# Gate projections cut into four parts over three attention passes, in place of two halves over two

## The chip, the cores and the metric

The kernel runs on one core of one Trainium2 chip. The metric is device microseconds (us), the median of three runs. TensorE is called PE below, VectorE DVE, ScalarE ACT, GpSimd POOL and SyncE SP.

## The reference, cut to what matters

Two transformer blocks in one launch: a first block with attention, a gated MLP mixer and a mixture of experts, and then a second block of two layers. The change stands in the token mixing of those two layers (`_token_mixing`, 256 tokens, width 1024):

```
proj = n @ w_in
nsa_q, nsa_kv, nsa_g, dil_qkv, fox_qkv, fox_f, merge_g = _split_cols(proj, IN_WIDTHS)
y_a = _nsa_attention(...)        # 4 heads: compressed, selected and windowed keys
y_b = _dilated_attention(...)    # 6 heads
y_c = _forgetting_attention(...) # 6 heads, scores plus a cumulated log gate
g_a, g_b, g_c = jnp.split(jax.nn.sigmoid(merge_g), 3, axis=-1)
merged = g_a * (y_a @ br_nsa) + g_b * (y_b @ br_dil) + g_c * (y_c @ br_fox)
return merged @ w_out
```

`merge_g` is 3 x 1024 columns of `n @ w_in`: the "gate units" below are the products that make it, 256 columns each, so 12 units in a layer. They need nothing of the attention, so they can stand between its steps.

## The kernel before

Every weight comes as a unit of 128 x 2048 float32 (1 MB) through a ring of three (`raw`, `whi`, `wlo`). SP loads a unit into `raw`; ACT rounds it (`conv_hi`, L278, `whi<-raw`); DVE subtracts to get the rest (`conv_lo`, L284, `wlo<-raw,whi`); PE then multiplies in three products, high by high, high by low and low by high (`mm3`, L357 to L359). A place of the ring can be converted anew once PE has used it (`unit_used`), and loaded anew once `conv_lo` has read it.

Each engine works through one list of instructions, written out by hand, in that order, and waits on semaphores. The part in question is the loop over 20 attention passes (one head each, both query tiles), with these steps for pass i:

- PE: scores of pass i into PSUM bank i % 2 (mask L2010, product L2016; the last six passes, those of the forgetting attention, have two more products, L2014), call it S(i); then three transposes of the exponentials of pass i-1 (L2025, T(i-1)), which wait for `exp2` of pass i-1; then the product with the values for pass i-2 (L2037, V(i-2)), which waits for `pt2_out`, ACT's copy of the transposed exponentials. Then the gate products of this pass, if any.
- DVE: the row maximum of pass i (L2423, R(i)); after it, in some passes, a `conv_lo`, or the closing arithmetic of a finished group of heads (`nsa_out` at 12, `dil_weights` at 15, `dil_out` at 18, `fox_out` at 19).
- ACT: the two exponentials of pass i (L2160, E(i)), which wait for R(i); in some passes the copy of a finished gate unit from bank 7 to its place (`gate_out`, L2102); the copy of the transposed pass i-1 (L2171); in some passes a `conv_hi`.

A gate unit is 48 products: two tiles of tokens, eight chunks of the depth, three products each. Six of the twelve units (numbers 5 to 10) stand in this loop and all use the one PSUM bank 7. A unit may start only when ACT has copied the unit before it out of the bank (`m_out`). The table of before and the waits around it:

```
ATT_GATES = {3 * (h // 2) + h % 2: (5 + h // 2, h % 2) for h in range(12)}
...
if tile == 0:
    pe.wait_ge(*(B["oc_out"].at(0, l) if f == 5 else B["m_out"].at(f - 1, l)))
gate_unit(f, 7, tile)
```

So three passes make a group: the first has 24 products of a unit, the second the other 24, the third none. ACT's `gate_out` and the conversion of the next unit (both engines) stand in the third pass of the group. After the loop come the last transposes of the outputs (`turn_two`, L1947), gate unit 11 in two halves, and the three branch products (units `BR0` to `BR0 + 2`).

Of the kernel before, what the change touches and what calls it, by code (L numbers as in the profile page):

```python
# [26 lines left out]
P = 128  # L27
# [3 lines left out]
DC = D // P  # L31
UNIT = 2048
RING = 3
# [93 lines left out]
def bass_network(nc, W, AD, x_in, ctx_in, s1_in, s2_in, k1_in, masks_in, gf_in, out):  # L127
    with ExitStack() as ctx:
# [17 lines left out]
        hhi = sb("hhi", [P, DC, S], F32R)  # L146
        hlo = sb("hlo", [P, DC, S], F32R)
# [23 lines left out]
        PS = ctx.enter_context(nc.psum_tensor("PS", [P, 8, 512], F32))  # L171
# [95 lines left out]
        def conv_hi(act, c, e=0):  # L267
            s = c % RING
            src = raw[:, s]
            if B1_UNITS <= c < LAYER0:  # L270
                m = c - B1_UNITS
                src = raw5[m % 5]
                act.wait_ge(landed5[m % 5], 16 * (m // 5 + 1))
            else:
                act.wait_ge(landed[s], e * 16 + 16 * ((c if c < LAYER0 else c - MOE_UNITS) // RING + 2))
            if not (isinstance(e, int) and c + 3 * e < RING):
                act.wait_ge(unit_used, e * 3 + (c - RING + 1))
            nc.scalar.activation(whi[:, s], src, ACT.Copy).then_inc(hi_ready, 1)  # L278

        def conv_lo(dve, c, e=0):  # L280
            s = c % RING
            dve.wait_ge(hi_ready, e * 3 + (c + 1))
            src = raw5[(c - B1_UNITS) % 5] if B1_UNITS <= c < LAYER0 else raw[:, s]
            nc.vector.tensor_tensor(wlo[:, s], src, whi[:, s].bitcast(F32), ALU.subtract).then_inc(lo_ready, 1)  # L284

        def unit(pe, c, e=0):
            pe.wait_ge(lo_ready, e * 3 + (c + 1))
            return whi[:, c % RING], wlo[:, c % RING]
# [66 lines left out]
        def mm3(out_, ah, al, bh, bl, start, stop, check=False):  # L355

            nc.tensor.matmul(out_, ah, bh, start=start, stop=False, skip_group_check=check)  # L357
            nc.tensor.matmul(out_, ah, bl, start=False, stop=False, skip_group_check=check)  # L358
            return nc.tensor.matmul(out_, al, bh, start=False, stop=stop, skip_group_check=check)  # L359
# [1508 lines left out]
        G = [qj[:, :, 256 * f:256 * f + 256] for f in range(5)] + [qj[:, :, C_FQ + 256 * f:C_FQ + 256 * f + 256] for f in range(3)]  # L1868
        G += [s1[:, 512 * f:512 * f + 512].rearrange("p (t n) -> p t n", t=2) for f in range(2)]
        G += [xn[:, :, 768:1024], oc_part.rearrange("p (t n) -> p t n", t=2)]  # L1870
        ATT_GATES = {3 * (h // 2) + h % 2: (5 + h // 2, h % 2) for h in range(12)}
        FF0, QK0 = LAYER0, LAYER0 + FFN_UNITS
        CM0 = QK0 + 15
        BR0 = QK0 + 26
# [1 line left out]
        CG = [QK0 + 12 + f + (2 if f >= 3 else 0) for f in range(12)]  # L1876
# [22 lines left out]
        def pe_layer(pe, l):  # L1899
# [35 lines left out]
            def gate_unit(f, bank, tile=None):  # L1935

                ins = project(unit(pe, CG[f], E0), hhi, hlo, bank, range(NT) if tile is None else (tile,))
                if tile != 0:
                    ins.then_inc(unit_used, 1)

            pe.wait_ge(*B["tb_act"].at(7, l))
# [63 lines left out]
            for i in range(PASSES2 + 2):  # L2005
                if i < PASSES2:
                    q, k, mk, _ = pass2(i)
                    if i >= 2:
                        pe.wait_ge(*B["exp2"].at(i - 2, l))
                    nc.tensor.matmul(PS[:, i % 2], idb[:, :], masks[:, mk], start=True, stop=False, skip_group_check=True)  # L2010
                    for t in range(NT):
                        o = PS[:, i % 2, 256 * t:256 * t + P * (t + 1)]
                        if i >= 14:
                            nc.tensor.matmul(o, fl[:, i - 14, t * P:(t + 1) * P], fr[:, 0:P * (t + 1)], start=False,  # L2014
                                             stop=False, skip_group_check=True)
                        ins = nc.tensor.matmul(o, q[:, t * P:(t + 1) * P], k[:, 0:P * (t + 1)], start=False, stop=t == 1,  # L2016
                                               skip_group_check=True)
                    ins.then_inc(*B["s2_mm"].up)
                if 1 <= i <= PASSES2:
                    p = i - 1  # L2020
                    pe.wait_ge(*B["exp2"].at(p, l))
                    if p >= 2:
                        pe.wait_ge(*B["pt2_out"].at(p - 2, l))
                    for n, c in enumerate((0, 256, 384)):
                        ins = nc.tensor.transpose(PS[:, 2 + p % 2, n * P:(n + 1) * P], pr2[:, p % 2, c:c + P], ident)  # L2025
                    ins.then_inc(*B["p2_turned"].up)
                if i >= 2:
                    p = i - 2
                    pe.wait_ge(*B["pt2_out"].at(p, l))
                    if p in (0, 4):  # L2030
                        pe.wait_ge(*B["m_out"].at(3 + p // 4, l))
                    if p == 12:
                        pe.wait_ge(*B["ya_done"].at(0, l))
                    bank, slot, v = FILL_BANK[p // 4], (p % 4) * 2, pass2(p)[3]
                    for t in range(NT):
                        for c in range(t + 1):
                            ins = nc.tensor.matmul(PS[:, bank, 64 * (slot + t):64 * (slot + t) + 64],  # L2037
                                                   pt2[:, p % 2, (t + c) * P:(t + c + 1) * P], qj[:, c, v:v + 64],
                                                   start=c == 0, stop=c == t)
                    ins.then_inc(*B["pv2"].up)  # L2040
                if i in ATT_GATES:
                    f, tile = ATT_GATES[i]
                    if tile == 0:
                        pe.wait_ge(*(B["oc_out"].at(0, l) if f == 5 else B["m_out"].at(f - 1, l)))
                    gate_unit(f, 7, tile)
                if i == PASSES2:
                    pe.wait_ge(*B["y2_made"].at(0, l))
                    turn_two(xn, 0, 6)
# [41 lines left out]
        def act_layer(act, l):  # L2090
# [8 lines left out]
            def gate_out(f, bank, conv=True):  # L2099

                act.wait_ge(unit_used, E0 * 3 + (CG[f] + 1))
                nc.scalar.activation(G[f], PS[:, bank].rearrange("p (t n) -> p t n", t=2), ACT.Copy).then_inc(*B["m_out"].up)  # L2102
                if conv:
                    conv_hi(act, CG[f] + RING, E0)
# [44 lines left out]
            for i in range(PASSES2 + 1):  # L2149
                if i < PASSES2:  # L2150
                    act.wait_ge(*B["negmax2"].at(i, l))
                    if i >= 2:
                        act.wait_ge(*B["p2_turned"].at(i - 2, l))
                    if i == 17:
                        act.wait_ge(*B["lse_sub"].at(0, l))
                        nc.scalar.activation(lw, lw, ACT.Exp).then_inc(*B["lse_exp"].up)
                    for t in range(NT):
                        n = 2 * i + t
                        o = slice(256 * t, 256 * t + P * (t + 1))
                        ins = nc.scalar.activation(pr2[:, i % 2, o], PS[:, i % 2, o], ACT.Exp, bias=nm2[:, n:n + 1],  # L2160
                                                   accum_out=den2[:, n:n + 1])
                    ins.then_inc(*B["exp2"].up)
                done = ATT_GATES.get(i - 1, (0, 0))
                if done[1]:
                    gate_out(done[0], 7, False)
                if i >= 1:
                    p = i - 1
                    act.wait_ge(*B["p2_turned"].at(p, l))
                    if p >= 2:
                        act.wait_ge(*B["pv2"].at(p - 2, l))  # L2170
                    nc.scalar.activation(pt2[:, p % 2, 0:384], PS[:, 2 + p % 2, 0:384], ACT.Copy).then_inc(*B["pt2_out"].up)  # L2171
                if done[1]:
                    conv_hi(act, CG[done[0]] + RING, E0)
            def split_hi(i, bank, dst):
                act.wait_ge(*B["y2_turned"].at(i, l))
                nc.scalar.activation(dst.rearrange("p c n -> p (c n)"), PS[:, bank], ACT.Copy).then_inc(*B["y2_hi"].up)
# [49 lines left out]
        def dve_layer(dve, l):  # L2226
# [194 lines left out]
            for i in range(PASSES2):  # L2421
                dve.wait_ge(*B["s2_mm"].at(i, l))
                nc.vector.tensor_reduce(nm2[:, 2 * i:2 * i + 2], PS[:, i % 2].rearrange("p (t n) -> p t n", t=2), AX.X, ALU.max,  # L2423
                                        negate=True).then_inc(*B["negmax2"].up)
                if i == 12:
                    nsa_out()
                done = ATT_GATES.get(i - 1, (0, 0))
                if done[1]:
                    conv_lo(dve, CG[done[0]] + RING, E0)
                if i == 15:  # L2430
                    dil_weights()
                if i == 18:
                    dil_out()
                if i == 19:
                    fox_out(14, 2, 4, 256)
# [306 lines left out]
```

## Time and profile before

| | |
|---|---|
| median of 3 runs | 2044.33 us (2043.84 to 2047.06) |
| the profiled execution, its own time | 2044.41 us |
| its span, first to last instruction | 2042.6 us |
| PE busy, of the span | 94% |
| DVE busy | 67% |
| ACT busy | 48% |
| mean granted PE clock | 0.975 |

PE is busy nearly all the time, so the total is PE's work and the few stretches in which it waits. In the rows further down a time is the start in us from the start of the span, and the number behind it is how long the merged piece lasted; the ends of matmuls are modelled and overlap the next start, so starts are what is compared. A square bracket gives the idle time of the engine ahead of the row and what ended it. "xN" is the count of merged instructions.

### The profile page before, as it was taken

How to read it: one execution, taken by the hardware profiler on the slowest of the kernel's cores; microseconds unless marked ns; L12 is line 12 of the kernel's file. 1: busy time of each engine (PE TensorE's matmuls, PEld its weight loads, DVE VectorE, ACT ScalarE, POOL GpSimd, SP SyncE). 2: the span in 40 equal slices, each digit the busy share in tenths (PEclk: the TensorE clock that was granted, in tenths of full speed). 3: DMA queues.
4: the chain of work that ended last, by engine and by line, in shares of the span. 5: the costliest groups of instructions: out<-in, count | busy, mean ns of one | idle time of the engine just before them, and what ended most of it. 6: DMA issues, size and time to landing. Idle time of an engine off the chain costs nothing.

```text
span 2042.6 us, 29838 instructions
## 1 busy us (share of the span) xinstructions
PE 1926.8 (94%) x12628; PEld 1717.0 (84%) x12656; DVE 1375.3 (67%) x1459; ACT 988.4 (48%) x1146; POOL 84.9 (4%) x107
## 2 busy tenths in 40 slices
PE   7999889999997999999998999999999999989998
PEld 3977678888886899899877899989998997779997
DVE  4889468898896777756336677678766462475444
ACT  3355457777775333454445533353335444444332
POOL 1330100000001000000000000000001000000000
PEclk9989989999998999999998999999999999899999
DMA  8556349999894687554321587748773542134554
GB/s 361 212 222 227 125 157 351 348 375 349 345 376 193 258 302 273 220 205 167 123 83 65 209 341 275 264 181 337 291 284 133 197 167 82 62 124 165 186 186 155
DMA packets 63878, 458.42 MB, mean 224 GB/s; under 512 B 7041, under 2 KB 7297, under 8 KB 8833
## 3 DMA queue, kind: packets, MB, share of 16 engines
q1 hardware_dynamic: 63744, 456.51, 59.1%
q8 instruction: 100, 1.64, 0.3%
q14 instruction: 34, 0.27, 0.0%
HBM read 455.43 MB, written 1.05 MB: 223 GB/s over the span
## 4 chain that ended last, share of the span: by engine, by line
issue 57%; PE 28%; DVE 9%; ACT 2%; DMA 1%; POOL 1%; DVEq 1%; POOLq 0%; ACTq 0%; SPq 0%
PE PS L357 8%; PE PS L359 7%; PE PS L358 7%; DVE acc L330 3%; DVE wlo L284 2%; PE PS L1253 1%; ACT whi L278 1%; PE PS L963 1%; DMA raw<-in_stream 1%; DMA ada<-in_ada 1%; POOL Z L489 1%; DVE hlo L466 0%; PE PS L935 0%; PE PS L1317 0%; DVE sm L1782 0%
## 5 line engine op out<-in xcount | busy, mean ns | idle before, releaser
L284 DVE TENSOR_TENSOR wlo<-raw,whi 128x2048 fp32r<-128x2048 f32 x282 | 646.8, 2296 | 349.2 <-ACT whi L278 344.0
L278 ACT ACTIVATE whi<-raw 128x2048 fp32r<-128x2048 f32 x282 | 538.5, 1912 | 359.1 <-PE PS L359 315.0
L357 PE MATMUL PS<-whi,hhi 128*128 128x256 f32 (+1 forms) x1568 | 504.8, 322 | 28.1 <-DVE wlo L284 13.3
L358 PE MATMUL PS<-wlo,hhi 128*128 128x256 f32 (+1 forms) x1568 | 493.1, 314 | 0.0
L359 PE MATMUL PS<-whi,hlo 128*128 128x256 f32 (+1 forms) x1568 | 492.9, 314 | 0.0
L357 PEld LDWEIGHTS PS<-whi,hhi 128*128 128x128 f32 x1568 | 304.8, 194 | 51.5 <-DVE wlo L284 14.9
L357 PE MATMUL PS<-hhi,whi 128*128 128x256 f32 x1152 | 326.7, 284 | 2.2 <-DVE mod L352 2.2
L359 PE MATMUL PS<-hhi,wlo 128*128 128x256 f32 x1152 | 326.0, 283 | 0.0
L358 PE MATMUL PS<-hlo,whi 128*128 128x256 f32 x1152 | 326.0, 283 | 0.0
L359 PEld LDWEIGHTS PS<-whi,hlo 128*128 128x128 f32 x1568 | 304.2, 194 | 16.8
L358 PEld LDWEIGHTS PS<-wlo,hhi 128*128 128x128 f32 x1568 | 305.0, 195 | 15.5
L357 PE MATMUL PS<-whi,zr 128*128 128x512 f32 (+2 forms) x672 | 248.4, 374 | 2.6 <-DVE wlo L284 2.6
L330 DVE SCALAR_TENSOR_TENSOR acc<-ada,cs,acc 128x512 f32<-128x512 f32 x308 | 239.3, 777 | 9.3 <-DMA ada<-in_ada 0.4
L359 PE MATMUL PS<-whi,zr 128*128 128x512 f32 (+2 forms) x672 | 243.6, 367 | 0.0
L358 PE MATMUL PS<-wlo,zr 128*128 128x512 f32 (+2 forms) x672 | 243.2, 366 | 0.0
L357 PEld LDWEIGHTS PS<-hhi,whi 128*128 128x128 f32 x1152 | 221.0, 192 | 4.6 <-DVE mod L352 3.5
L358 PEld LDWEIGHTS PS<-hlo,whi 128*128 128x128 f32 x1152 | 221.0, 192 | 1.1
L359 PEld LDWEIGHTS PS<-hhi,wlo 128*128 128x128 f32 x1152 | 221.0, 192 | 0.0
L357 PEld LDWEIGHTS PS<-whi,zr 128*128 128x128 f32 (+1 forms) x672 | 121.4, 181 | 25.9 <-issue 4.1
L359 PEld LDWEIGHTS PS<-whi,zr 128*128 128x128 f32 (+1 forms) x672 | 121.3, 180 | 22.8
L358 PEld LDWEIGHTS PS<-wlo,zr 128*128 128x128 f32 (+1 forms) x672 | 121.5, 181 | 20.7
L284 DVE TENSOR_TENSOR wlo<-ada,whi 128x2048 fp32r<-128x2048 f32 x48 | 109.8, 2291 | 14.6 <-ACT whi L278 14.4
(394 smaller groups left out, 1775.7 us busy)
## 6 DMA issues: line engine op xcount, KB each, us to landing
raw<-in_stream SPq DMA_DIRECT2D x285, 1024.0 KB, 4.8
ada<-in_ada SPq DMA_DIRECT2D x92, 1024.0 KB, 4.9
ada<-in_stream SPq DMA_DIRECT2D x48, 1024.0 KB, 4.9
raw<-in_ada SPq DMA_DIRECT2D x3, 1024.0 KB, 15.6
xs<-in_x SPq DMA_DIRECT2D x1, 1024.0 KB, 11.8
Z<-in_ada SPq DMA_DIRECT2D x1, 1024.0 KB, 19.6
Z<-in_ctx SPq DMA_DIRECT2D x1, 1024.0 KB, 10.7
masks<-in_masks SPq DMA_DIRECT2D x2, 512.0 KB, 9.8
```

The costliest lines, as they stand in the source:

```text
L278: nc.scalar.activation(whi[:, s], src, ACT.Copy).then_inc(hi_ready, 1)
L284: nc.vector.tensor_tensor(wlo[:, s], src, whi[:, s].bitcast(F32), ALU.subtract).then_inc(lo_ready, 1)
L330: ins = nc.vector.scalar_tensor_tensor(a, w, c, a, ALU.mult, ALU.add)
L357: nc.tensor.matmul(out_, ah, bh, start=start, stop=False, skip_group_check=check)
L358: nc.tensor.matmul(out_, ah, bl, start=False, stop=False, skip_group_check=check)
L359: return nc.tensor.matmul(out_, al, bh, start=False, stop=stop, skip_group_check=check)
L489: nc.gpsimd.tensor_tensor(diag, mid(ident, [P, DC, P]), bc(gcol[:, :], [P, DC, P]), ALU.mult).then_inc(*N.diag.up)
L963: ins = nc.tensor.matmul(PS[:, X_BANK[c // 4], (c % 4) * P:(c % 4 + 1) * P], xn[:, t, c * P:(c + 1) * P], pick[:, b, t], start=t == 0, sto ...
L1253: ins = nc.tensor.matmul(PS[0:2, bank, :], cs[:, n:16:8], slot[:, 512 * k:512 * k + 512], start=n == 0, stop=n == 7)
```

## The change

The 48 products of a gate unit are cut into four parts of 12 (one tile, four chunks of the depth). The first pass of a group of three gets two parts, the second one, the third one. ACT's `gate_out` with its conversion, and DVE's conversion, move with the end of the unit: they stand in the pass after the third, which is the first pass of the next group.

```
-        ATT_GATES = {3 * (h // 2) + h % 2: (5 + h // 2, h % 2) for h in range(12)}
+        GATE_PARTS = {3 * u + p: [(5 + u, q) for q in ((0, 1), (2,), (3,))[p]] for u in range(6) for p in range(3)}
+        GATE_DONE = {3 * u + 2: 5 + u for u in range(6)}
...
+            def gate_part(f, q):
+
+                wh, wl = (w.rearrange("p (k n) -> p k n", k=DC) for w in unit(pe, CG[f], E0))
+                t = q // 2
+                for k in range(4 * (q % 2), 4 * (q % 2) + 4):
+                    ts = slice(t * P, (t + 1) * P)
+                    ins = mm3(PS[:, 7, t * 256:(t + 1) * 256], hhi[:, k, ts], hlo[:, k, ts], wh[:, k], wl[:, k], k == 0, k == DC - 1)
+                if q == 3:
                     ins.then_inc(unit_used, 1)
...
-                if i in ATT_GATES:
-                    f, tile = ATT_GATES[i]
-                    if tile == 0:
+                for f, q in GATE_PARTS.get(i, ()):
+                    if q == 0:
                         pe.wait_ge(*(B["oc_out"].at(0, l) if f == 5 else B["m_out"].at(f - 1, l)))
-                    gate_unit(f, 7, tile)
+                    gate_part(f, q)
...
-                done = ATT_GATES.get(i - 1, (0, 0))
-                if done[1]:
-                    gate_out(done[0], 7, False)
+                done = GATE_DONE.get(i - 1)
+                if done:
+                    gate_out(done, 7, False)
...
-                if done[1]:
-                    conv_hi(act, CG[done[0]] + RING, E0)
+                if done:
+                    conv_hi(act, CG[done] + RING, E0)
...
-                done = ATT_GATES.get(i - 1, (0, 0))
-                if done[1]:
-                    conv_lo(dve, CG[done[0]] + RING, E0)
+                done = GATE_DONE.get(i - 1)
+                if done:
+                    conv_lo(dve, CG[done] + RING, E0)
```

On PE, from the third pass of the first group (mask, scores, transposes, values) up to the gate products of the pass after it. Before:

```order
4653 L2010 MATMUL PS<-masks,idb 128x512
4654 L2016 MATMUL PS<-Z 128x128
4655 L2016 MATMUL PS<-Z 128x256
4656 L2025 MATMUL PS<-k,ada 128x128 x3
4657 L2037 MATMUL PS<-Z,ada 128x64 x3
4658 L2010 MATMUL PS<-masks,idb 128x512
4659 L2016 MATMUL PS<-Z 128x128
4660 L2016 MATMUL PS<-Z 128x256
4661 L2025 MATMUL PS<-k,ada 128x128 x3
4662 L2037 MATMUL PS<-Z,ada 128x64 x3
4663 L357 MATMUL PS<-whi,hhi 128x256
```

And of the change (its lines are 11 further down; behind row 4646 stand the other eleven products of the part):

```order
4641 L2021 MATMUL PS<-masks,idb 128x512
4642 L2027 MATMUL PS<-Z 128x128
4643 L2027 MATMUL PS<-Z 128x256
4644 L2036 MATMUL PS<-k,ada 128x128 x3
4645 L2048 MATMUL PS<-Z,ada 128x64 x3
4646 L357 MATMUL PS<-whi,hhi 128x256
...
4658 L2021 MATMUL PS<-masks,idb 128x512
4659 L2027 MATMUL PS<-Z 128x128
4660 L2027 MATMUL PS<-Z 128x256
4661 L2036 MATMUL PS<-k,ada 128x128 x3
4662 L2048 MATMUL PS<-Z,ada 128x64 x3
4663 L357 MATMUL PS<-whi,hhi 128x256
```

Twelve products now stand between the third pass and the next one; the row at which the next unit starts is the same, 4663.

On ACT, from the exponentials of pass 2 (L2160, two for each pass, then the copy L2171). Before:

```order
385 L2160 ACTIVATE ada,sm<-PS,sm 128x128
386 L2160 ACTIVATE ada,sm<-PS,sm 128x256
387 L2102 ACTIVATE Z<-PS 128x2x256
388 L2171 ACTIVATE ada<-PS 128x384
389 L278 ACTIVATE whi<-raw 128x2048
390 L2160 ACTIVATE ada,sm<-PS,sm 128x128
391 L2160 ACTIVATE ada,sm<-PS,sm 128x256
392 L2171 ACTIVATE ada<-PS 128x384
```

And of the change (L2170 the exponentials, L2112 `gate_out`, L2181 the copy):

```order
385 L2170 ACTIVATE ada,sm<-PS,sm 128x128
386 L2170 ACTIVATE ada,sm<-PS,sm 128x256
387 L2181 ACTIVATE ada<-PS 128x384
388 L2170 ACTIVATE ada,sm<-PS,sm 128x128
389 L2170 ACTIVATE ada,sm<-PS,sm 128x256
390 L2112 ACTIVATE Z<-PS 128x2x256
391 L2181 ACTIVATE ada<-PS 128x384
392 L278 ACTIVATE whi<-raw 128x2048
```

`gate_out` of the first unit moved behind the exponentials of pass 3, the pass in which PE starts the next unit in the same bank.

On DVE, the end of the loop: the maxima of passes 16 and 17 (L2423), the last conversion, the maximum of 18 and `dil_out` (L2390 to L2408), then the maximum of 19. Before:

```order
573 L2423 TENSOR_REDUCE sm<-PS 128x2 x2
574 L284 TENSOR_TENSOR wlo<-raw,whi 128x2048
575 L2423 TENSOR_REDUCE sm<-PS 128x2
576 L2390 TENSOR_TENSOR sm<-sm,acc 128x12
...
582 L2408 TENSOR_TENSOR xn<-Z 128x2x2x64
583 L2423 TENSOR_REDUCE sm<-PS 128x2
```

And of the change:

```order
571 L2433 TENSOR_REDUCE sm<-PS 128x2 x3
572 L284 TENSOR_TENSOR wlo<-raw,whi 128x2048
573 L2400 TENSOR_TENSOR sm<-sm,acc 128x12
...
579 L2418 TENSOR_TENSOR xn<-Z 128x2x2x64
580 L2433 TENSOR_REDUCE sm<-PS 128x2
```

The conversion moved from ahead of the maximum of pass 18 to behind it, so that it and `dil_out` now both stand between the maxima of passes 18 and 19.

## Rows read from the trace of the kernel before

**Rows 1.** Whole span: busy time of each engine, from the page.

```profile
PE 1926.8 (94%) x12628; PEld 1717.0 (84%) x12656; DVE 1375.3 (67%) x1459; ACT 988.4 (48%) x1146; POOL 84.9 (4%) x107
```

**Rows 2.** PE's waits, 985 to 1095 us (first layer): total, times, longest.

```profile
PE PS L2025 <- ACT ada L2160: 6.6, 6, 2.0
```

**Rows 3.** PE in order of time, passes 3 to 6, gate products but the first left out.

```profile
1004.58 0.36 PE L357 MATMUL PS<-whi,hhi 128*128 128x256 f32 x1
...
1007.87 0.92 PE L2016 MATMUL PS<-Z 64*128 64x128 f32 x4 [0.16 <-issue]
1009.57 0.55 PE L2025 MATMUL PS<-k,ada 128*128 128x128 f32 x3 [0.78 <-ACT ada L2160]
...
1013.60 0.39 PE L2010 MATMUL PS<-masks,idb 128*128 128x512 bf16 x1
1013.91 0.92 PE L2016 MATMUL PS<-Z 64*128 64x128 f32 x4
1014.76 0.55 PE L2025 MATMUL PS<-k,ada 128*128 128x128 f32 x3
1015.15 0.78 PE L2037 MATMUL PS<-Z,ada 128*128 128x64 f32 x6
1016.08 0.92 PE L2016 MATMUL PS<-Z 64*128 64x128 f32 x4
1016.92 0.55 PE L2025 MATMUL PS<-k,ada 128*128 128x128 f32 x3
1017.43 0.88 PE L2037 MATMUL PS<-Z,ada 128*128 128x64 f32 x6
1018.12 0.36 PE L357 MATMUL PS<-whi,hhi 128*128 128x256 f32 x1
```

**Rows 4.** ACT in order of time: exponentials of pass 3, then pass 5 with its followers.

```profile
1008.60 0.37 ACT L2160 ACTIVATE ada<-PS,sm 128x128 f32<-128x128 f32 x1 [2.96 <-DVE sm L2423]
...
1015.60 0.37 ACT L2160 ACTIVATE ada<-PS,sm 128x128 f32<-128x128 f32 x1 [4.52 <-DVE sm L2423]
...
1016.40 0.59 ACT L2102 ACTIVATE Z<-PS 128x512 f32<-128x512 f32 x1
1016.88 0.50 ACT L2171 ACTIVATE ada<-PS 128x384 f32<-128x384 f32 x1
1017.25 1.93 ACT L278 ACTIVATE whi<-raw 128x2048 fp32r<-128x2048 f32 x1
```

**Rows 5.** DVE in order of time, maxima of passes 3, 5 and 6.

```profile
1007.88 0.68 DVE L2423 TENSOR_REDUCE sm<-PS 128x2 f32<-128x512 f32 x1
...
1014.87 0.69 DVE L2423 TENSOR_REDUCE sm<-PS 128x2 f32<-128x512 f32 x1 [5.36 <-PE PS L2016]
1019.21 2.29 DVE L284 TENSOR_TENSOR wlo<-raw,whi 128x2048 fp32r<-128x2048 f32 x1 [3.65 <-ACT whi L278]
1021.42 0.68 DVE L2423 TENSOR_REDUCE sm<-PS 128x2 f32<-128x512 f32 x1
```

**Rows 6.** PE in order of time, passes 16 and 18 to the branch products.

```profile
1065.75 0.55 PE L2025 MATMUL PS<-k,ada 128*128 128x128 f32 x3
...
1075.08 0.55 PE L2025 MATMUL PS<-k,ada 128*128 128x128 f32 x3
...
1080.32 0.90 PE L2025 MATMUL PS<-k,ada 128*128 128x128 f32 x3 [1.96 <-ACT ada L2160]
...
1083.90 0.90 PE L2025 MATMUL PS<-k,ada 128*128 128x128 f32 x3 [1.51 <-ACT ada L2160]
...
1092.68 0.36 PE L357 MATMUL PS<-whi,hhi 128*128 128x256 f32 x1
```

**Rows 7.** DVE in order of time, passes 18 and 19.

```profile
1078.63 0.68 DVE L2423 TENSOR_REDUCE sm<-PS 128x2 f32<-128x512 f32 x1
1079.23 0.16 DVE L2390 TENSOR_TENSOR sm<-sm,acc 128x12 f32<-128x12 f32 x1
...
1082.21 0.68 DVE L2423 TENSOR_REDUCE sm<-PS 128x2 f32<-128x512 f32 x1
```

**Rows 8.** Stretches: us, busy time of each engine, PE's granted clock, DMA.

```profile
991.00:995.00 4.00, 4.00 (x19) 4.00 (x20) 1.41 (x2) 0.91 (x4) 0.00 (x0) 0.52 0.50 172
...
1083.90:1092.70 8.80, 8.80 (x52) 8.80 (x52) 2.10 (x4) 4.45 (x7) 0.00 (x0) 0.63 0.00 0
...
1112.00:1120.00 8.00, 3.43 (x20) 2.14 (x19) 7.85 (x15) 3.99 (x5) 0.00 (x0) 1.00 0.00 1
```

**Rows 9.** PE's waits, 1680 to 1790 us (second layer).

```profile
PE PS L2025 <- ACT ada L2160: 6.8, 6, 2.0
```

More of the change, by code:

```diff
@@ L1938, in gate_unit @@
                 if tile != 0:
+                    ins.then_inc(unit_used, 1)
+            def gate_part(f, q):
[5 more added lines that the diff above has]
+                if q == 3:
                     ins.then_inc(unit_used, 1)
```

## The prediction, made before the changed kernel ran

> **What bounds the kernel now.** I read the page first: PE is busy 94% of the span [rows 1], so time is gained or lost only where PE waits, or where its products run at a lower clock. Then PE's waits around the attention loop of the first layer: it waits six times for ACT's exponentials, 6.6 us in all [rows 2], and the second layer shows the same six, 6.8 us [rows 9]. No wait there is for a transfer. So in this stretch the order of the three lists decides, and I walked it in order of time.
>
> In the groups of passes 3 to 14 one wait comes once per group, in its second pass: 0.78 us ahead of the transposes of pass 3, in pass 4 [rows 3]. Its cause is the conversion on DVE. The one in pass 5 starts at 1019.21 and holds back the maximum of pass 6 until 1021.42 [rows 5], though those scores were done by about 1017.00 (row 1016.08 + 0.92 [rows 3]). The last two waits, 1.96 and 1.51 us, come in passes 19 and 20, which have no gate products at all [rows 6].
>
> **The times used.** From start to start:
> - S, the scores: 13.60 to 14.76, 1.16 us; T, the transposes: 14.76 to 15.15, 0.39; V, the values: 15.15 to the next mask product, 0.61 (the mask stands 0.31 ahead of row 1016.08) [rows 3].
> - 24 gate products at full clock: first one at 1004.58, next mask at 1007.87 - 0.31 = 1007.56, so 2.98 us, about 24 x 0.12 + 0.10. V ahead of gate products takes 1018.12 - 1017.43 = 0.69, which is 0.08 more than ahead of a mask [rows 3]. A further block of gate products thus costs about 0.16 us of switching, the products themselves being the same.
> - End of scores to maximum: 0.04 (1013.91 + 0.92 = 1014.83, then 1014.87). Maximum to exponentials: 1015.60 - 1014.87 = 0.73. Exponentials to the next ACT instruction: 0.80. `gate_out`: 0.59 and some 0.05 until PE sees it, 0.64. `gate_out` to the copy 0.48, copy to `conv_hi` 0.37, copy to V 1017.43 - 1016.88 = 0.55. Start of `conv_hi` to `conv_lo` 1019.21 - 1017.25 = 1.96, `conv_lo` to the next maximum 2.21 [rows 3 to 5]. Exponentials to T: 1009.57 - 1008.60 = 0.97 [rows 3, 4].
>
> Walked with these, the list of before gives a group of 13.53 us; the trace has 1018.12 - 1004.58 = 13.54 [rows 3]. The walk also puts the last T of the loop at 1083.8 against 1083.90 [rows 6]. That is why I trust it with the new list.
>
> **The change part by part, in one layer.**
>
> 1. What goes: the wait for the late maximum. In the walk it is 0.88 us a group (from the end of S's slot; the trace shows 0.78 as idle [rows 3]), and 0.12 that V waits for the copy behind `gate_out` (1017.43 - 1016.92 = 0.51 against 0.39 [rows 3]). In the new list the conversion starts one pass later, behind 24 gate products, and ends 0.2 to 0.3 us behind the next scores, so the maximum is hardly late; and 12 products stand between it and the transposes that need it. Four groups (passes 3 to 14) have this wait: -1.00 each. The fifth (15 to 17) has none, since its scores are longer: T in pass 16 starts at 1065.75 with no wait [rows 6].
>
> 2. What comes: the handover of bank 7. The first 12 products of a unit wait until `gate_out` of the unit before is done, and that now stands behind the exponentials of the same pass. From the end of the scores: 0.04 + 0.73 + 0.80 + 0.64 = 2.21 us. PE needs T and V in between, 0.39 + 0.61, less the 0.07 by which it is already past the modelled end of the scores: 0.93. It stands still for 1.27 us, at five places (units 6 to 10). Queued behind it is the next pass's scores, so the pipeline of DVE and ACT stands too. Before, this copy was done in the third pass, and a whole pass with no gate products hid it.
>
> 3. What comes: a third block of gate products in each of six groups, 0.16 us each.
>
> 4. What moves at the end of the loop. The conversion stood ahead of the maximum of pass 18; now it stands behind it, and ahead of `dil_out` (1079.23 to 1082.21, 2.98 us [rows 7]) and the maximum of 19. Before, from the start of T(17) at 1075.08 to T(19) at 1083.90: 8.82 us [rows 6]; the walk has 8.86. New, from the same point: scores end and maximum 0.11, exponentials 0.73, `gate_out` 0.80, copy 0.48, `conv_hi` 0.37, `conv_lo` 1.96, `dil_out` 2.21, maximum of 19 2.98, exponentials 0.73, T(19) 0.97, sum 11.34. That is 2.48 us more, and PE has nothing left to do in it: one wait of 7.1 us where before there were two of 1.96 and 1.51.
>
> 5. The transfers: each load is issued when `conv_lo` frees its place, so it comes later by what the loop loses, and a group of 14 us has one. No wait of PE here was for one. Cost 0. If the cover were gone, PE would wait at a unit's start for `conv_lo`, and the branch products would be late first.
>
> 6. The clock at the end. Before, PE comes back from the last waits at half clock: granted 0.63 over 1083.9 to 1092.7 [rows 8]. The new wait is longer, but the work behind it is the same, so I take the same cost, 0 more; between 3.3 us less in each layer (all of it at full clock, 8.80 x (1 - 0.63)) and 1.4 us more (twelve more products at half clock, 0.12 us each on top).
>
> Sum of a layer: opening group 0.16; four groups (1.27 + 0.16 - 1.00) x 4 = 1.72; fifth group 1.43; end 2.48. Together 5.79 us. What follows (branch products, their gating, the output) starts from PE's last products of the loop, so it moves as a whole. Two layers: 11.6 us. Against the profiled execution's own 2044.41 us, which is within 0.1 us of the median 2044.33, this gives **2056.0 us**.
>
> **The rivals.**
>
> *The short waits cost the clock too* (chance 0.09). Then each of the ten handovers lets the clock fall to its lower level. The price of one, from the 24 products behind pass 0, which ran at 0.52 of the clock in 991 to 995 [rows 8]: 4 us there do what 2.1 would at full clock, 1.9 us lost. Ten of them are 19 us: 2075. Against it stands the stretch 1112 to 1120, in which PE was busy 3.43 of 8 us and the granted clock stayed 1.00 [rows 8]; the same loop of before keeps 1.00 through its 0.78 us waits. The Trainium skill, "TensorE: Matmul & The Clock Gate", section "A second HAM failure mode: psum-queue depth-cycling", speaks for this rival: frequent small idles between groups of matmuls at a PSUM handover made the clock swing there. By that rule the time would be 2075; by the stretch 1112 to 1120 it is 2056.
>
> *The end of the loop costs nothing more* (0.07). If the wait in pass 20 were covered, only 3.31 us a layer are left: 2051.0. For it speaks only that this part of the walk is the longest; against it, that DVE's list has no other order.
>
> *Faster: the handover is free* (0.03). If bank 7 were copied out before PE comes to it, the groups win the 1.00 us wait in full. Items 1 and 3 alone are (-4.00 + 0.96) x 2 = -6.1 us, 2038.3, and with the end of the loop 2043.3. It decides below a handover of about 0.2 us (ten of them against 6.1 - 4.1 = 2.0 us) with no loss at the end, against 1.27 worked out; with the end's loss in, it cannot reach the bound. The same page, section "HAM oscillation — how this bites in real kernels", reports that a second PSUM buffer brought its kernel nothing worth having, so that a single one cost nothing; by that the sum is 2043.3. There the products of a group were not waiting for an engine that stood behind another's chain, as here; no row of before shows a handover that PE waits for, so this is untested.
>
> **How the numbers follow.** The likeliest case, 2056, has 0.81. Its own range: the clock at the end gives -6.6 to +2.8 over both layers, the switching at 0 instead of 0.16 gives -1.9; a clock wholly regained behind a longer wait is unlikely, so about 2050 to 2060. For 8 in 10 I take 2050 to 2062: the lower end takes in the second rival, the upper one handovers that lose the clock once or twice (1.9 each). A measurement of this kernel can tell about 0.2%, 4 us, from no change. Faster has 0.03, the same (2040 to 2048) has 0.05, from a cheap handover with the end's loss, slower has 0.92.
>
> **What would show it.** In the profile of the changed kernel PE waits for `gate_out` (L2112) ahead of L357 some ten times, 1.2 to 1.3 us each, and the 0.78 us waits ahead of the transposes are gone in passes 4, 7, 10 and 13. A group takes about 14.0 us from first gate product to first gate product. In pass 20 PE waits about 7 us. DVE has the conversion and `dil_out` back to back. The prediction is wrong if the granted clock falls inside the loop, if the handover wait is under 0.8 us, or if the stretch behind the loop comes out shorter.

## The result, and the profile after

The changed kernel takes 2062.82 us (median of 6 runs, 2061.12 to 2063.86) against 2044.94 for the kernel before: a ratio of 1.0083, 95% interval 1.0073 to 1.0092, or 17.9 us more where 11.6 were forecast. The median stands 0.8 us above the upper end of the stated range, 2062; the ratio applied to the 2044.33 us from which the forecast started gives 2061.3, just inside. All medians in this document are of the fast executions: one slow one of a3_both (2141.7 us) and one of the kernel before (6600.0 us) are left out. The profiled execution took 2061.12 us, its span 2059.3, which is 16.7 more than before. The lines below are of the changed kernel unless a sentence says otherwise; line numbers are ten or eleven higher (L2036 the transposes, L2112 `gate_out`, L2170 the exponentials, L2433 the maximum).

The page, busy time of each engine over the span, as in [rows 1]:

```profile
PE 1935.6 (94%) x12656; PEld 1722.8 (84%) x12656; DVE 1375.5 (67%) x1459; ACT 989.4 (48%) x1146; POOL 84.9 (4%) x107
```

PE was busy for 8.8 us more with the same products. The trace of before lacks 28 of the records (x12628 against x12656), which at 0.12 us each hide at most 3.4 us of it; the rest must be products that ran longer. PE's waits from 985 to 1100 us, the loop of layer 0 (who waited for whom: total, times, longest):

```profile
PE PS L2036 <- ACT ada L2170: 7.0, 1, 7.0
PE PS L357 <- ACT Z L2112: 3.4, 3, 1.1
PE PS L357 <- ACT s L2112: 2.2, 2, 1.1
```

The six waits of [rows 2] are gone; there are now one of 7.0 us ahead of the transposes and five of 1.1 us ahead of the gate products, for `gate_out` (`Z` and `s` are the two places to which it copies). The second layer shows the same lines. PE in order of time, pass 6 and the start of the next unit, the counterpart of [rows 3]:

```profile
1016.02 0.39 PE L2021 MATMUL PS<-masks,idb 128*128 128x512 bf16 x1
1016.34 0.92 PE L2027 MATMUL PS<-Z 64*128 64x128 f32 x4
1017.19 0.55 PE L2036 MATMUL PS<-k,ada 128*128 128x128 f32 x3
1017.58 0.78 PE L2048 MATMUL PS<-Z,ada 128*128 128x64 f32 x6
1019.48 0.38 PE L357 MATMUL PS<-whi,hhi 128*128 128x256 f32 x1 [1.12 <-ACT Z L2112]
...
1033.21 0.38 PE L357 MATMUL PS<-whi,hhi 128*128 128x256 f32 x1 [1.12 <-ACT Z L2112]
```

ACT in the same pass, as in [rows 4]:

```profile
1018.02 0.37 ACT L2170 ACTIVATE ada<-PS,sm 128x128 f32<-128x128 f32 x1 [2.36 <-DVE sm L2433]
...
1018.83 0.59 ACT L2112 ACTIVATE Z<-PS 128x512 f32<-128x512 f32 x1
1019.31 0.50 ACT L2181 ACTIVATE ada<-PS 128x384 f32<-128x384 f32 x1
```

The copy out of bank 7 ends at 1019.42, and PE starts the next unit at 1019.48. A group takes 1033.21 - 1019.48 = 13.73 us, against 13.54 before. The end of the loop on DVE, as in [rows 7], and on PE, as in [rows 6]:

```profile
1077.45 0.69 DVE L2433 TENSOR_REDUCE sm<-PS 128x2 f32<-128x512 f32 x1 [4.00 <-PE PS L2027]
1081.79 2.29 DVE L284 TENSOR_TENSOR wlo<-raw,whi 128x2048 fp32r<-128x2048 f32 x1 [3.65 <-ACT whi L278]
1084.00 0.16 DVE L2400 TENSOR_TENSOR sm<-sm,acc 128x12 f32<-128x12 f32 x1
...
1086.99 0.68 DVE L2433 TENSOR_REDUCE sm<-PS 128x2 f32<-128x512 f32 x1
```

```profile
1080.55 0.55 PE L2036 MATMUL PS<-k,ada 128*128 128x128 f32 x3
1080.93 0.78 PE L2048 MATMUL PS<-Z,ada 128*128 128x64 f32 x6
1088.67 0.69 PE L2036 MATMUL PS<-k,ada 128*128 128x128 f32 x2 [6.96 <-ACT ada L2170]
```

Maximum of pass 18, conversion, `dil_out`, maximum of pass 19 stand one behind the other, and PE is idle for 6.96 us. Ahead of the conversion DVE is itself idle for 3.65 us, until ACT's `conv_hi` is done.

Laid over the kernel before by landmarks on PE, the 16.7 us of span stand as in the table. The landmark behind each loop is the start of the second half of gate unit 11, 1092.68 us before; [rows 6] calls that row the branch products, but they follow only at 1095.63.

| stretch | before | after | difference |
|---|---|---|---|
| start to the first scores of layer 0 | 989.35 | 989.69 | +0.34 |
| loop of layer 0, to the transposes of pass 19 | 94.55 | 98.98 | +4.43 |
| from there to the second half of unit 11 | 8.78 | 8.00 | -0.78 |
| second half of unit 11 to the first scores of layer 1 | 588.69 | 595.64 | +6.95 |
| loop of layer 1, to the transposes of pass 19 | 94.90 | 100.70 | +5.80 |
| from there to the second half of unit 11 | 9.00 | 8.97 | -0.03 |
| the rest | 257.33 | 257.32 | -0.01 |

The largest single entry is a stretch in which nothing was changed. Its two ends cut a little closer, at waits with the same place in the code (columns: stretch, its length, then busy time and count of PE, PEld, DVE, ACT, POOL, the granted PE clock, DMA share and GB/s). Before:

```profile
1113.94:1678.93 564.99, 546.89 (x4019) 513.52 (x4023) 399.09 (x422) 244.05 (x231) 14.83 (x20) 1.00 0.65 242
```

After:

```profile
1117.94:1689.39 571.45, 553.95 (x4023) 519.80 (x4023) 399.27 (x422) 244.06 (x231) 14.87 (x20) 0.99 0.64 240
1765.00:1770.00 5.00, 4.39 (x24) 4.39 (x24) 2.23 (x1) 2.74 (x4) 0.00 (x0) 0.66 0.01 3
```

PE idles for 18.1 us in the one and 17.5 in the other; its busy time is 7.1 us longer, with four records missing in the first, worth some 0.5 us. DVE and ACT are as before. The granted clock is lower, 0.99 against 1.00. The second line is a place inside the loop of layer 1, behind a handover, where it fell too. What happens in the unchanged stretch shows at one wait. Before:

```profile
1148.83 0.39 PE L357 MATMUL PS<-whi,hhi 128*128 128x256 f32 x1 [2.23 <-DVE wlo L284]
1149.05 0.28 PE L358 MATMUL PS<-wlo,hhi 128*128 128x256 f32 x1
```

After:

```profile
1154.83 0.57 PE L357 MATMUL PS<-whi,hhi 128*128 128x256 f32 x1 [2.23 <-DVE wlo L284]
1155.19 0.42 PE L358 MATMUL PS<-wlo,hhi 128*128 128x256 f32 x1
```

The same wait, of the same 2.23 us, for the same conversion. Before, the products behind it take 0.28 us each, after it 0.42: 2.4 GHz there, 1.2 GHz here. In the changed kernel the granted clock falls so at four places of this stretch (about 1120, 1154, 1175 and 1574 us); in the traced execution of before it stays up throughout.

One execution of each kernel is traced, and the clock differs between executions too. The 989 us ahead of the first loop are the same code in all fourteen traced kernels, and they take from 989.0 us (b2_shift12, b3_conv_later) to 994.6 us (a1_copy_first). The kernel before took from 2043.5 to 2051.8 us in the groups of runs below, at mean granted clocks from 0.975 down to 0.970; the traced one, 2044.4 us at 0.975, is among its shorter ones.

### The profile page after: what moved, and what is told of

Read it like the earlier page. It is cut to its first block, busy times and chain, and to the rows that moved or that the text cites. A ratio compares the mean times of both kernels' runs of the same rounds, so it can differ in the third digit from the quotient of the medians.

```text
span 2059.3 us, 29866 instructions
## 1 busy us (share of the span) xinstructions
PE 1935.6 (94%) x12656; PEld 1722.8 (84%) x12656; DVE 1375.5 (67%) x1459; ACT 989.4 (48%) x1146; POOL 84.9 (4%) x107
## 4 chain that ended last, share of the span: by engine, by line
issue 57%; PE 28%; DVE 9%; ACT 2%; DMA 1%; POOL 1%; DVEq 1%; POOLq 0%; ACTq 0%; SPq 0%
PE PS L357 8%; PE PS L359 7%; PE PS L358 7%; DVE acc L330 3%; DVE wlo L284 2%; PE PS L1253 1%; ACT whi L278 1%; PE PS L963 1%; DMA raw<-in_stream 1%; DMA ada<-in_ada 1%; POOL Z L489 1%; PE PS L1317 0%; DVE hlo L466 0%; PE PS L935 0%; DVE sm L1782 0%
```

## The experiments

Theory: the change costs what the three queues say (handover, end of the loop), and the rest is the clock behind unchanged waits, lost because the change moved them (**P**). Rivals: the queues' part is something else (the experiments on the changed kernel), or the lost clock belongs to the changed loop itself (**Q**). A third possibility, that the clock behind these waits differs from one execution to the next whatever the edit, was not tested by an experiment of its own; the medians over several executions bear on it. All medians are compared with the kernel before on the same chip, 2046.0 to 2046.5 us in these groups.

**a1_copy_first**: in the changed kernel, ACT copies bank 7 out ahead of the exponentials.

```
             for i in range(PASSES2 + 1):
+                done = GATE_DONE.get(i - 1)
+                if done:
+                    gate_out(done, 7, False)
                 if i < PASSES2:
                     act.wait_ge(*B["negmax2"].at(i, l))
...
-                done = GATE_DONE.get(i - 1)
-                if done:
-                    gate_out(done, 7, False)
```

> The changed kernel, but ACT's gate_out stands ahead of the exponentials of its pass (it is ready then: the unit's last products end before that pass's scores). Theory 1 (the handover of bank 7 is late because it stands behind the exponentials, which wait for the maximum): the five 1.12 us waits ahead of the gate products vanish in each layer, a group falls from 13.73 to about 12.4 us, and the copy to V comes 0.48 us earlier; by the walk some 6.5 us a layer, 13 in all, so 2048 to 2050 us with the clock as in the changed kernel. Theory 2 (the wait is a matter of PE's own start of a block of products, or of the bank): the waits stay and the time stays near 2062. The 7 us wait at the end of the loop stays in both.

Measured: 2043.0 us (2039.5 to 2049.5, 10 runs), ratio 0.9985 (0.9975 to 0.9995). PE's waits from 985 to 1100 us:

```profile
PE PS L2036 <- ACT ada L2173: 6.5, 1, 6.5
PE PS L2012 <- ACT Z L2157: 1.1, 1, 1.1
```

All handover waits are gone, and the long one is left. Theory 1 holds, and the gain, some 20 us, is more than the 13 worked out; the time is 5 us under the 2048 to 2050 expected. The profiled execution was one of the longest (2048.7) because its first scores came at 994.62 us and not at 989.69. From there to its end it took 17.4 us less than the changed kernel: 6.9 in the loop of layer 0, where 6.5 were worked out, 8.2 in that of layer 1, where no handover loses the clock any more, and 1.8 behind it.

**a2_conv_last**: in the changed kernel, DVE's last conversion behind `fox_out`.

```
-                if done:
+                if done and i != 18:
                     conv_lo(dve, CG[done] + RING, E0)
...
                 if i == 19:
                     fox_out(14, 2, 4, 256)
+                    conv_lo(dve, CG[10] + RING, E0)
```

> The changed kernel, but DVE's last conversion of the loop (that for the unit freed by unit 10) stands behind fox_out of pass 19 instead of ahead of dil_out in pass 18. Theory 1 (the 6.96 us wait in pass 20 is the conversion and dil_out in front of the maximum of pass 19): the wait shrinks to 1 to 2 us, about 6 us less in each layer, 2049 to 2051 us; PE may then keep full clock there, up to 2 us less again in each layer. Theory 2 (dil_out itself waits for something else): the wait stays above 4 us. The 1.12 us waits stay in both.

Measured: 2047.6 us (2043.3 to 2048.8, 10 runs), ratio 1.0007 (0.9998 to 1.0017), so 15 us less than the changed kernel, 1.4 under the 2049 to 2051 expected. The wait in pass 20 is 1.0 us, and the clock stays up behind the loop of layer 0, as the expectation allowed for. Theory 1 holds.

**a3_both**: the two edits together.

> Both edits in the changed kernel: gate_out first, last conversion last. If the two costs are apart and add up, some 25 us less than the changed kernel, 2036 to 2039 us, under the kernel before (2044.9), since the parts also take away its 0.78 us waits. If one hides the other, not below 2045.

Measured: 2034.6 us (2033.7 to 2035.5, three executions), ratio 0.9943 (0.9923 to 0.9963). That is below the kernel before, as expected, and 1.4 us under the 2036 to 2039 worked out. The two gains measured alone, 20 and 15 us, don't add up to the 28 of both; the walk had 25 for both. How much the clock has in each median isn't seen.

**b1_shift33, b2_shift12, b5_shift57**: the kernel before, with extra products into bank 7 at the end of the first loop, n = 11, 4 and 19. Unit 11 writes the bank anew right after.

```
             pe.wait_ge(*B["m_out"].at(10, l))
+            if l == 0:
+                wh, wl = (w.rearrange("p (k n) -> p k n", k=DC) for w in unit(pe, CG[11], E0))
+                for _ in range(n):
+                    mm3(PS[:, 7, 0:256], hhi[:, 0, 0:P], hlo[:, 0, 0:P], wh[:, 0], wl[:, 0], True, True)
             gate_unit(11, 7, 0)
```

> The kernel before, with 33 more gate products (three by three into bank 7, overwritten by unit 11 right after, so the output is unchanged) at the end of the loop of layer 0 only: 33 x 0.12 = 3.96 us of pure PE work, which moves all that follows by the amount by which the changed kernel had moved it (3.99 us). Theory P (the five half-clock stretches that only the changed kernel has, behind its first loop at 1120, 1154, 1174 and 1574 us and at a handover in layer 1, come of where the same small waits now fall): this kernel shows such new stretches too, four of them behind the first loop, and takes 3.96 and some 5 to 7 us more, 2054 to 2056. Theory Q (they come of the changed loop, its longer waits): none of them appears and the time is 2048.4 to 2049.

> The kernel before with 12 extra gate products (1.44 us at full clock) at the end of the loop of layer 0 only, overwritten right after. Theory P (what matters is where the unchanged waits behind the loop fall): the time doesn't follow the added work; it is 2047.5 if none of the waits loses the clock, and up to 7 us more if some do, and the four waits behind the loop (1126, 1157, 1369 and 1577 us with 33 products) need not be the ones that do. Theory Q (added work costs itself, and the 33 products' excess of 5.6 us was something fixed, set off by any edit there): 2047.5 and the same excess, 2053.

> The kernel before with 57 extra gate products (6.84 us at full clock) at the end of the loop of layer 0 only. Theory P: the time is not monotone in the added work. Between 33 and 57 products all later work moves by 2.88 us, and the four new half-clock stretches, worth some 5.6 us, can go again: about 2046.0 + 6.8 = 2053, less than the 2055.6 of 33 products in spite of 24 more. Theory Q: at least 2055.6 + 2.9 = 2058.5.

Measured, with the unchanged stretch between the same two waits as above (its position: start of the transposes behind it, less that of L2001 or L2012 just ahead of the first loop):

| kernel | added work | median | over the kernel before | position | stretch |
|---|---|---|---|---|---|
| before | 0 | 2046.0 to 2046.5 | 0 | 127.40 | 564.99 |
| b2_shift12 | 1.44 | 2050.3 | 3.8 | 128.87 | 571.15 |
| b1_shift33 | 3.96 | 2055.6 | 9.6 | 131.34 | 571.14 |
| changed kernel | | 2062.8 | 17.9 | 131.42 | 571.45 |
| b5_shift57 | 6.84 | 2052.8 | 6.3 | 134.19 | 564.97 |

The stretch of b1_shift33 and that of b5_shift57, with the same columns as above:

```profile
1119.80:1690.94 571.14, 553.32 (x4023) 519.22 (x4023) 399.13 (x422) 244.19 (x231) 14.86 (x20) 0.99 0.64 240
```

```profile
1120.92:1685.89 564.97, 546.84 (x4020) 513.50 (x4024) 399.17 (x422) 244.22 (x231) 14.85 (x20) 1.00 0.65 242
```

In these medians 57 products more cost less than 33 more, but the intervals of the two ratios overlap (1.0020 to 1.0042 and 1.0029 to 1.0062); that the unchanged stretch is not monotone is read from the traces. Two things do not hang on one execution: b1_shift33 pays at least 5.9 us, the lower end of its interval, for 3.96 us of work, and no execution of b5_shift57 (2050.3 to 2055.8) comes near Q's 2058.5. Of b2_shift12 the 2050.3 us lie within P's wide 2047.5 to 2054.5 and under Q's 2053. Not one instruction behind the added products differs between these kernels, and the waits of the stretch have the same lengths, but for 0.3 us less at its start in b2_shift12, as in the changed kernel. So work that only displaces the later code is enough to make waits of that code lose the clock, as P says.

The falls of b2_shift12 are those of the changed kernel: granted 0.50 behind the same four waits. In both kernels, the second and the last of the four:

```profile
1152.00:1155.00 3.00, 3.00 (x14) 3.00 (x15) 2.29 (x1) 1.15 (x1) 0.55 (x1) 0.50 0.62 210
1572.00:1575.00 3.00, 3.00 (x15) 3.00 (x16) 2.29 (x1) 1.15 (x1) 0.45 (x1) 0.50 0.66 229
```

```profile
1155.00:1158.00 3.00, 3.00 (x15) 3.00 (x16) 2.29 (x1) 1.15 (x1) 0.51 (x1) 0.50 0.69 229
1575.00:1578.00 3.00, 3.00 (x15) 3.00 (x16) 2.29 (x1) 1.15 (x1) 0.44 (x1) 0.50 0.79 229
```

The position in the table does not decide it alone. b1_shift33 and the changed kernel stand at 131.34 and 131.42, and only two of their four falls are at the same waits: b1_shift33 has the others at 1126 and 1369 us. a1_copy_first, at 124.53, falls at the same four waits as b1_shift33. The moment of a fall moves too: at the 2.23 us wait in b1_shift33 the clock falls some 0.8 us behind its end, in the changed kernel at about the moment at which PE comes back. PE in order of time in b1_shift33:

```profile
1156.31 0.38 PE L357 MATMUL PS<-whi,hhi 128*128 128x256 f32 x1 [2.23 <-DVE wlo L284]
1156.53 0.28 PE L358 MATMUL PS<-wlo,hhi 128*128 128x256 f32 x1
...
1157.12 0.41 PE L357 MATMUL PS<-whi,hhi 128*128 128x256 f32 x1
1157.33 0.41 PE L358 MATMUL PS<-wlo,hhi 128*128 128x256 f32 x1
```

**c1_after_shift24**: the changed kernel with eight times three such products.

> The changed kernel with 24 extra gate products (2.88 us) at the end of the loop of layer 0 only. All later work then stands about where it does in the kernel before with 57. Theory P: the stretches at 1120, 1154, 1175 and 1574 us go, and with more work it is faster than the changed kernel: 2062.8 + 2.9 - 6 to 8 = 2058 to 2060 us. Theory Q (the changed loop itself makes them): 2065.7.

Measured: 2065.3 us (2064.9 to 2067.5, 4 runs), which is what Q gave. P's 2058 to 2060 missed, and the trace says why it is a poor test: a handover inside its first loop lost the clock (1062 to 1068 us, the granted clock is the third value from the end):

```profile
1062.00:1068.00 6.00, 5.12 (x28) 4.93 (x28) 2.63 (x3) 3.01 (x5) 0.00 (x0) 0.72 0.00 0
```

So the stretch came to stand at 136.74 and not near 134.2, the place of b5_shift57, as meant. It took 569.86 us, with four falls again. This leaves open whether the changed kernel could be put back to 565.

**b3_conv_later**: the kernel before, with DVE's conversions one pass later alone (`ATT_GATES.get(i - 2, ...)` in DVE's list).

> The kernel before with one thing of the change alone: DVE's conversion one pass later (behind the maximum of the next group's first pass; at the end behind the maximum of pass 18). ACT and PE as before. By the walk the 0.78 us waits in passes 4, 7, 10 and 13 go (3.4 us a layer) and nothing comes in the groups, since the gate copy stays in the third pass; at the end the maximum of pass 19 gets later by 0 to 1 us, as the conversion's input is ready earlier than in the changed kernel. So the second half of the change, not the cut of the products, holds its gain: the start of unit 11 some 3 us a layer earlier, 2039 to 2041 us if the clock behaves as before, up to 7 us more if waits behind the loop lose it.

Measured: 2044.0 us, ratio 0.9987 (0.9978 to 0.9997). PE's waits from 985 to 1100 us:

```profile
PE PS L2025 <- ACT ada L2160: 3.9, 1, 3.9
```

The 0.78 us waits are gone and one of 3.9 us in pass 20 is left, in place of 1.96 and 1.51. The gain is 2.5 us and not 5 to 7: in the trace the two loops are 4.5 and 4.9 us shorter, but the unchanged stretch takes 569.81 us (1109.38 to 1679.19), 4.8 more than before, and the code behind the second loop 2.9 more. The expectation had named that loss as possible, up to 7 us.

**b4_conv_last**: the kernel before, with only the last conversion behind `fox_out` (the edit of a2_conv_last). **d3_two_halves**: both DVE edits, b3_conv_later and b4_conv_last, still with halves of 24.

> The kernel before with its last conversion of the loop behind fox_out of pass 19 alone; the conversions of the groups stay where they were. The waits of 1.96 and 1.51 us in passes 19 and 20 shrink to 0 and some 1.2 us, and with so short a wait the clock stays up behind the loop: by the walk 2.3 us a layer from the waits and 1 to 2.6 us a layer from the clock, 2036 to 2040 us, unless the waits behind the loop come to lose the clock (up to 6 us back). The 0.78 us waits stay. With b3_conv_later (2044.0) and d3_two_halves (2028.0) it shows which of the two edits carries the gain.

> The kernel before (unit in two halves of 24, none in the third pass) with DVE's conversion one pass later and the last one behind fox_out of pass 19: what a3_both has without the cut of the products and without moving the gate copy. By the walk its loop is as short as that of a3_both, within 0.3 us a layer (a group of 12.6 us, the wait in pass 20 1.2 us). If the cut in four parts is worth nothing of itself, it takes the same 2035 us, up to 5 us either way by where the later waits fall; if the cut helps, it is more than that slower, with waits left in its groups.

Measured: b4_conv_last 2036.6 us, ratio 0.9954 (0.9942 to 0.9966), inside its 2036 to 2040, with the 0.78 us waits still there and one of 1.0 us in pass 20; d3_two_halves 2028.0 us (2023.5 to 2033.2), ratio 0.9902 (0.9882 to 0.9922), the lowest median of all, from four executions that lie in two pairs (2023.5 and 2024.4, 2031.7 and 2033.2). PE's waits in d3_two_halves, 985 to 1100 us:

```profile
PE PS L2016 <- issue: 1.1, 5, 0.5
PE PS L2001 <- ACT Z L2147: 1.1, 1, 1.1
PE PS L2025 <- ACT ada L2160: 1.0, 1, 1.0
```

No wait for another engine is left in the groups, and the unit was never cut. Its median is 7 us under that of a3_both, a little beyond the 5 that were allowed for. The traces show that this is not the loops: a group takes 12.57 us here and 12.40 in a3_both, and the loops are 0.5 and 1.1 us longer here (86.84 and 87.56 us, against 86.33 and 86.49). The 0.17 us of a group come of the copy and not of the cut: here V still waits some 0.2 us for its copy behind `gate_out` in the third pass, while a3_both has `gate_out` ahead of the exponentials and pays for one block of products more. So the cut into four shows no worth of its own. The traced execution of d3_two_halves is its longest, 2033.2 us; what the two shortest did differently isn't seen, and the 7 us stay unexplained.

**d1_both_plus5, d2_conv_last_plus5**: a3_both and a2_conv_last, with five single products (0.60 us) at the end of the loop of layer 0.

> a3_both with five extra gate products (0.60 us of pure PE work, overwritten right after) at the end of the loop of layer 0. Theory P: the kernel before runs the code from the first wait behind its loop to the last one ahead of the loop of layer 1 in 565.0 us, b5_shift57 too, and the same code takes 569.3 us in a3_both, because two of its waits lose the clock. Moved by 0.6 us a3_both comes to stand like the kernel before (by b5 and before, positions that far apart are alike), so those two half-clock stretches (1140 and 1560 us) go: 0.6 more work, 4.3 less lost, 2031 to 2032 us. Theory Q (the stretches belong to the loop's edits): 2035.6.

> a2_conv_last with the same five extra products. Theory P: its stretches at 1144, 1164 and 1564 us go, 569.3 becomes 565.0: 2047.6 + 0.6 - 4.3 = 2043.9 us, if the stretches in and behind the loop of layer 1, which also move, stay as they are. Theory Q: 2048.2.

Measured: d1_both_plus5 2032.4 us (2028.5 to 2036.7), ratio 0.9933 (0.9918 to 0.9948), against 0.9943 (0.9923 to 0.9963) for a3_both: the intervals overlap. The fall at 1140 us is gone, and one at 1161 that the expectation hadn't counted; the one at 1560 is still behind the same wait, and a new one appears at 1351 us. The part between the landmarks takes 567.97 us, not 565.0. d2_conv_last_plus5 took 2049.1 us (2039.7 to 2053.5): P's 2043.9 missed, and Q's 2048.2 is nearer. Its profiled execution was its fastest, 2039.7, so what its typical run did is not seen. One kernel, with all its code in one place, thus spreads over 14 us: the place of a wait within the kernel is not all that decides whether it loses the clock, and the time can't be steered by a fraction of a microsecond of work.

## Why the prediction was right in its direction and short in its size

*Item 1, the late maximum goes.* Right: the waits ahead of the transposes are gone from the groups, and b3_conv_later shows that moving the conversion on DVE does that by itself.

*Item 2, the handover of bank 7.* Right in mechanism, place and number: five a layer, 1.12 us as idle time. On the measure of the walk, which had 1.27, it is 1.29: V starts at 1017.58, the products at 1019.48, and V itself has 0.61. The 1.2 to 1.3 us announced as idle time in the profile mixed the two measures. a1_copy_first takes it away by one moved instruction.

*Item 3, a third block of products.* Mis-sized: a part of twelve takes 1.51 us from its start to the next mask (1010.86 to 1012.37), and V ahead of it 0.59, no more than ahead of a mask: the 0.69 of [rows 3] was V's wait for its copy behind `gate_out` and no switching. So a block costs about 0.07 and not 0.16. A group grew by 0.19 (13.54 to 13.73) where 0.43 was worked out. It takes 12.57 with the late maximum gone (d3_two_halves) and 12.40 with four parts and the copy first (a3_both), so the change took away 0.97 of late maximum and some 0.2 that V waited for its copy, where the walk had 0.12, and it put in 1.33 of handover. The loop of a layer grew by 4.43 where the sum had 5.79.

*Item 4, the end of the loop.* Right: from the transposes of pass 17 (1077.35) to those of pass 19 (1088.67) 11.32 us, worked out 11.34; before it was 8.82 [rows 6]. a2_conv_last takes it away.

*Item 5, the transfers.* Right: no wait in the loops is for one.

*Item 6, the clock behind the loop.* Inside its bounds: -0.78 and -0.03 us. In layer 0 this is the shorter stretch that the prediction had named as a sign that it was wrong; so was a fall of the clock inside the loop, and one came, in layer 1.

*The step that failed* is the sentence ahead of the sum: "What follows (...) starts from PE's last products of the loop, so it moves as a whole." It moved, and took 6.95 us longer on the way. The queues' part of the 16.7 us is 2 x 4.43 = 8.9; the clock has nearly all the rest, 6.95 in the unchanged stretch and 1.4 in the loop of layer 1 (5.80 - 4.43). The prediction thus put 2.7 us too much on the loops and nothing on the clock behind unchanged waits, which took about 8.3. The two errors have opposite signs, and that the total came out near the range is in part luck. That added work alone can make waits of unchanged code lose the clock is shown on the kernel before: b1_shift33 pays 9.6 us for 3.96 us of work. That the displacement did so in the changed kernel itself is argued, from b2_shift12 with the same four falls and nearly the same length of the stretch (571.15 and 571.45): c1_after_shift24 did not undo it, and what differs from one execution to the next was not told apart.

*The rival on the clock* was right in kind and wrong in place. Of ten handovers one lost the clock (at 1765.61 us; from the start of the 24 products behind it to the next mask 4.47 us, elsewhere 2.97, so 1.5 us and not the 1.9 put on one), while 1.12 us waits at the nine other places did not. The Trainium skill, "TensorE: Matmul & The Clock Gate", section "A second HAM failure mode: psum-queue depth-cycling", has short idles between groups of matmuls, as PE cycles through PSUM banks, as what makes the clock swing; at the handovers this trace agrees once in ten. The greater loss came behind waits that the change had not touched. The rival on the other side, a free handover, fell: PE waited at all ten places. What the prediction said there of the waits in the page's kernel, that its products did not wait for an engine behind another's chain, the page does not state.

## What to carry to other kernels

Before a step is moved to "the next pass", look at what stands ahead of it there in each engine's own list: here a copy went behind the exponentials that wait for this pass's scores, and a conversion went between two maxima, and both lay on PE's path; the cover for the late maximum was to be had by moving DVE's conversion alone (b3_conv_later, and with the last conversion behind `fox_out` d3_two_halves). In a kernel in which PE waits in many places for 1 to 2 us, a change of a few microseconds early on can gain or lose as much again in code that it doesn't touch; add some idle-free work at the same place of the kernel before, in two or three sizes, and see by how much the time of the untouched part swings, before a small gain or loss is put down to the edit. Compare too how long the code ahead of every edit took in each trace: here that alone differed by 5.6 us.

## What the runs showed of the hardware

The same 2.23 us wait is followed by products of 0.28 us in one kernel and of 0.41 to 0.42 us in another, with the same code around it; the granted clock is 1.00 there and 0.50 here. Over the unchanged stretch of 565 us this makes steps of up to 6.5 us, and they do not grow with the added work: with 1.44, 3.96 and 6.84 us more of PE's work ahead of it the stretch took 571.15, 571.14 and 564.97 us. Over the whole kernel the medians rose by 3.8, 9.6 and 6.3 us. The executions of the kernel before and of b5_shift57 are the only ones of those traced in which no wait of this stretch lost the clock. The 989 us of the same code at the start took from 989.0 to 994.6 us. What decides which waits lose the clock was not found.
